# A two-block transformer kernel on one core: how five norm stages are computed, and what TensorE does while it waits in them

## Chip, core and metric

One Trainium2 core. The time is the device time of one execution in microseconds (us), the median of several. The kernel is one hand-scheduled program: each engine has its own instruction list, and all synchronisation is by counting semaphores.

## The reference, cut to what matters

Two blocks of two layers each, on 256 tokens ("LAT") of 1024 features, and from the second block on also on 256 context tokens. Every layer is: RMS norm, input projection, attention, output projection added to the tokens; then RMS norm, a wide feed-forward (2 x 2816 columns, a convolution over the tokens, a gate), and a down projection added to the tokens. What the change touches is the norm:

```python
y = x * rsqrt(mean(x * x) + eps) * g          # block 1 and its two layers
y = rms_norm(x, g) * (1 + scale) + shift      # block 2
```

All arithmetic is fp32. Each matrix product is made of three: both factors are split into a rounded part ("high") and the rest ("low"), and TensorE adds high*high, high*low and low*high.

## The kernel before

Weights stream from HBM in tiles of 1 MB into a ring of three slots. SyncE (SP) issues the transfers; the transfer into a slot waits until TensorE has read what was there. Each slot is handled in halves of 128 x 1024: ScalarE rounds a half into one of four high buffers (L334, helper `ahead`), GpSimd then writes the rest over the raw weights in place (L341), TensorE waits for that (L314) and multiplies (L347 to L349).

Five norms have no separate transposition stage and are called fronts here: the first layer's attention norm ("1.0 norm", behind the setup), "1.0 norm2", "1.1 norm", "1.1 norm2" and "2.1 norm2". All work on the two LAT tiles. A front runs like this:

- TensorE transposes the raw tokens into PSUM banks 4 to 7 (`turn_x_T`, L421; in the setup `first_T`, L1879). Feature tile k of 8 lies at `turned_k(k)`: 128 features by 256 tokens.
- ScalarE sums the squares of each token in two halves and takes two square roots (L464), one column per token tile; VectorE adds the first sum and eps before that (L437).
- TensorE spreads the two columns of roots over the 128 partitions, by a product with the identity into bank 3 (L430).
- VectorE inverts that 128 x 256 square (L439) into SBUF ("spread").
- For each k, VectorE multiplies bank, gain and spread into one of two SBUF buffers `TMP` (L446), ScalarE rounds that to the high part (L469; with a shift L471), and VectorE subtracts to get the low part (L454; with a shift L456). In order on VectorE: features 0, features 1, low 0, features 2, low 1, and so on. ScalarE also converts weight halves between these (`ahead` at L473 and L475).
- TensorE begins the next stage with k = 0 as soon as low 0 is there and waits for every low k in its first pass. In the feed-forward (`up_T`, L1226) this first pass is 48 products of 256 columns for two weight halves at once; in the projections (`in_T`) it is one column cut, half by half.

TensorE's instruction list is in program order; whatever stands in it ahead of a product is done before it. In the setup, SP issues the first three weight tiles, the gains, then 25 small loads (L2501) and the context tokens; ScalarE issues the identity and the tokens. The fourth weight tile waits for TensorE's reading of the first slot, and behind it on SP stand 16 small transfers (L1951) before the fifth tile.

## Time and profile before

| | us |
|---|---|
| median of 3 runs (1991.78 to 1992.41) | 1992.14 |
| the profiled execution | 1989.65 |
| its span, first to last instruction | 1987.9 |
| PE (TensorE matmul) busy | 1815.2 (91%) |
| POOL (GpSimd) / ACT (ScalarE) / DVE (VectorE) busy | 937.0 / 878.6 / 734.7 |
| mean granted TensorE clock, as a share of full speed | 0.942 |

The profiled execution is 2.49 us under the median of the three runs and its span 1.75 us under its own time. Busy time counts an engine with any instruction in flight; what an engine waited for is in the rows that follow below. The page also has the granted clock in 40 slices: it is 9 tenths or more in 36 of them.

### The profile page before, as it was taken

Reading aid. Unit: us, or ns where it says so; the run is one execution under the profiler, and the core shown is the slowest. Engines: PE = TensorE matmul, PEld = TensorE weight load, DVE = VectorE, ACT = ScalarE, POOL = GpSimd, SP = SyncE. Lnnn points to the kernel's source line nnn. Section 1 sums busy time; section 2 is a strip of 40 time slices with the busy share of each in tenths; the row PEclk is TensorE's granted clock in tenths of the full one; section 3 lists DMA queues with packets and bytes.
Section 4 is the critical chain, followed back from the end, with each engine's and each line's share of the span. In section 5 each row is a group of like instructions: output and inputs, shape, how many; then the busy total and the mean of one; then the engine's idle time right before and its main releaser. Section 6 shows DMA issues by size and latency. Waiting matters only on the chain.

```text
span 1987.9 us, 25834 instructions
## 1 busy us (share of the span) xinstructions
PE 1815.2 (91%) x10196; PEld 1463.2 (74%) x10196; DVE 734.7 (37%) x1591; ACT 878.6 (44%) x1542; POOL 937.0 (47%) x408
## 2 busy tenths in 40 slices
PE   5898999989789999789789999999999798889998
PEld 4667887867578878678544577888878686669986
DVE  4433223145432222464455425344311343344431
ACT  3655444345644443333324534444422255556653
POOL 3644676865356657333102023444434161138876
PEclk9999999999889999899875999999999899999999
DMA  5425997543169964222100022333323431126654
GB/s 192 148 86 182 305 308 264 170 149 127 64 208 304 307 240 166 69 85 85 43 0 1 1 85 64 88 103 99 92 80 105 102 106 43 43 85 170 182 160 146
DMA packets 257402, 261.36 MB, mean 131 GB/s; under 512 B 11123, under 2 KB 201811, under 8 KB 251011
## 3 DMA queue, kind: packets, MB, share of 16 engines
q1 hardware_dynamic: 256867, 258.61, 41.2%
q8 instruction: 81, 1.33, 0.3%
q10 hardware_dynamic: 416, 1.11, 0.1%
q14 instruction: 38, 0.31, 0.0%
HBM read 258.66 MB, written 1.05 MB: 131 GB/s over the span
## 4 chain that ended last, share of the span: by engine, by line
PE 78%; DVE 8%; ACT 5%; DMA 5%; issue 2%; POOL 1%; SPq 1%; ACTq 0%; DVEq 0%
PE bank L347 21%; PE bank L348 20%; PE bank L349 20%; PE bank L1382 2%; PE bank L719 2%; PE bank L1031 2%; PE bank L742 2%; ACT weights_high L334 1%; ACT work L1149 1%; PE bank L1001 1%; PE bank L1733 1%; DMA work<-in_ada_w 1%; PE bank L727 1%; DVE work L1110 1%; DMA weights<-in_hyb_w_in 1%
## 5 line engine op out<-in xcount | busy, mean ns | idle before, releaser
L341 POOL TENSOR_TENSOR weights_low<-weights,weights_high 128x1024 fp32r<-128x1024 f32 (+1 forms) x388 | 918.5, 2384 | 939.4 <-ACT weights_high L334 938.9
L334 ACT ACTIVATE weights_high<-weights 128x1024 fp32r<-128x1024 f32 (+1 forms) x388 | 401.0, 1045 | 477.1 <-PE bank L349 143.1
L347 PE MATMUL bank<-normed_features_high,weights_high 128*128 128x256 f32 (+1 forms) x1408 | 444.7, 316 | 13.3 <-DVE normed_features_low L454 6.7
L348 PE MATMUL bank<-normed_features_high,weights_low 128*128 128x256 f32 (+1 forms) x1408 | 439.4, 312 | 0.0
L349 PE MATMUL bank<-normed_features_low,weights_high 128*128 128x256 f32 (+1 forms) x1408 | 439.3, 312 | 0.0
L347 PE MATMUL bank<-weights_high,normed_features_high 128*128 128x512 f32 (+4 forms) x752 | 294.1, 391 | 34.9 <-POOL weights_low L341 10.8
L347 PEld LDWEIGHTS bank<-normed_features_high,weights_high 128*128 128x128 f32 x1408 | 272.2, 193 | 65.6 <-issue 35.4
L349 PEld LDWEIGHTS bank<-normed_features_low,weights_high 128*128 128x128 f32 x1408 | 272.0, 193 | 14.0
L348 PEld LDWEIGHTS bank<-normed_features_high,weights_low 128*128 128x128 f32 x1408 | 272.3, 193 | 13.6
L348 PE MATMUL bank<-weights_high,normed_features_low 128*128 128x512 f32 (+4 forms) x752 | 278.5, 370 | 0.0
L349 PE MATMUL bank<-weights_low,normed_features_high 128*128 128x512 f32 (+4 forms) x752 | 278.4, 370 | 0.0
L347 PEld LDWEIGHTS bank<-weights_high,normed_features_high 128*128 128x128 f32 x752 | 148.6, 198 | 70.8 <-issue 23.5
L347 PE MATMUL bank<-weights_high,hidden_high 128*128 128x512 f32 x440 | 175.6, 399 | 3.5 <-DVE hidden_low_narrow L1280 2.2
L349 PE MATMUL bank<-weights_low,hidden_high 128*128 128x512 f32 x440 | 173.0, 393 | 0.0
L349 PEld LDWEIGHTS bank<-weights_low,normed_features_high 128*128 128x128 f32 x752 | 148.5, 197 | 21.6
L348 PEld LDWEIGHTS bank<-weights_high,normed_features_low 128*128 128x128 f32 x752 | 149.1, 198 | 17.2
L1289 DVE SCALAR_TENSOR_TENSOR qk_features<-bank,convcol,qk_features 128x255 f32<-128x255 f32 x88 | 42.4, 482 | 213.1 <-ACT qk_features L1269 211.5
L347 PEld LDWEIGHTS bank<-weights_high,hidden_high 128*128 128x128 f32 x440 | 83.9, 191 | 28.9 <-DVE hidden_low_narrow L1280 4.7
L348 PE MATMUL bank<-weights_high,hidden_low_narrow 128*128 128x512 f32 x264 | 104.7, 397 | 0.0
L349 PEld LDWEIGHTS bank<-weights_low,hidden_high 128*128 128x128 f32 x440 | 83.9, 191 | 18.3
L583 DVE TENSOR_TENSOR bank<-bank,gate_rows 128x512 f32<-128x512 f32 x20 | 13.9, 696 | 209.5 <-PE bank L349 209.5
L1275 ACT ACTIVATE hidden_high<-bank 128x256 fp32r<-128x256 f32 (+1 forms) x88 | 38.6, 438 | 114.4 <-DVE bank L1318 81.0
(296 smaller groups left out, 2054.1 us busy)
## 6 DMA issues: line engine op xcount, KB each, us to landing
work<-in_ada_w SPq DMA_DIRECT2D x48, 1024.0 KB, 8.2
weights<-in_ffn_w_up SPq DMA_DIRECT2D x44, 1024.0 KB, 6.2
weights<-in_ffn_up SPq DMA_DIRECT2D x44, 1024.0 KB, 6.0
weights<-in_ffn_w_down SPq DMA_DIRECT2D x20, 1024.0 KB, 5.0
weights<-in_ffn_down SPq DMA_DIRECT2D x20, 1024.0 KB, 5.0
weights<-in_diff_w_qkv SPq DMA_DIRECT2D x12, 1024.0 KB, 5.1
weights<-in_hyb_w_in SPq DMA_DIRECT2D x11, 1024.0 KB, 5.4
weights<-in_odd_w_in SPq DMA_DIRECT2D x9, 1024.0 KB, 5.3
```

The source lines that it names most:

```text
L334: A.eng.activation(high(whigh[:, m % HIGHS, :]), raw(wslot[:, u % SLOTS, :]), ACT.Copy).then_inc(scalar_done, A.one(("A", "high", m)))
L341: G.eng.tensor_tensor(raw(wlow[:, u % SLOTS, :]), raw(wslot[:, u % SLOTS, :]), high(whigh[:, m % HIGHS, :]).bitcast(F32), ALU.subtract).th ...
L347: T.eng.matmul(out_, lh, rh, start=first, stop=False)
L348: T.eng.matmul(out_, ll, rh, start=False, stop=False)
L349: return T.eng.matmul(out_, lh, rl, start=False, stop=last)
L719: i = T.eng.matmul(bank[:, a:b], l, r, start=(m == 0), stop=(m == len(terms) - 1))
L727: i = T.eng.transpose(psum[3 + q % 2][:, c * P:(c + 1) * P], PB[q % NB][:, c * P:(c + 1) * P], ident)
L742: i = T.eng.matmul(o, l, r, start=(first and c == 0), stop=(last and c == nc_ - 1))
L1031: i = T.eng.matmul(psum[SCORES[x]][:, a:b], l, r, start=(m == 0), stop=(m == len(terms) - 1))
L1275: A.eng.activation(hidh(f, n), up_hidden(ph, f, n), ACT.Copy).then_inc(scalar_done, A.one(("A", ph, "high", f)))
L1289: V.eng.scalar_tensor_tensor(out=c[:, back:n], in0=g[:, 0:n - back], scalar=tap(2 - back, f), in1=c[:, back:n], op0=ALU.mult, op1=ALU.add) ...
L1382: i = T.eng.matmul(psum[4 + g][32 * j:32 * j + 2 + 2 * layer, :], (silu_below if layer else silu_c)[:, k, :], w[:, j * 512:(j + 1) * 512], ...
```

## The change

Three things, and one of the setup's loads:

- The two columns of roots are inverted first, by VectorE on 128 x 2 ("inverse"), and TensorE spreads the inverses. What VectorE then does with the square is a copy instead of an inversion. TensorE's spreading waits for VectorE instead of ScalarE.
- The features stay in the banks: VectorE writes the product back to `turned_k(k)`, and rounding and subtraction read it there. `TMP` is no longer used in fronts, and the wait for low k - 2 goes.
- TensorE multiplies the identity by itself into a bank that nobody reads: 5 products (2 in the setup) ahead of the wait for the inverse and 8 behind the spreading, plus 5 and 6 around the transposes of the setup.
- In the setup the tokens come in two transfers, one ahead of the weights on SP and one on ScalarE's queue, and ScalarE converts the first weight half right after the roots, the next three after k = 1, 3 and 5 (before: after k = 0, 2, 4 and 6).

```diff
+        def warm_T(T, bank, count):
+            for _ in range(count):
+                T.eng.matmul(psum[bank][:, 0:P], ident, ident, start=True, stop=True)
 def front_T(T, ph, x_ph):
             if x_ph != "setup":
                 turn_x_T(T, ph, x_ph, 1)
-            T.eng.wait_ge(scalar_done, done("A", ph, "root"))
+            if x_ph not in ("setup", "1.0 ffn down", "1.1 ffn down"):
+                T.eng.wait_ge(scalar_done, done("A", x_ph, "squares", 1))
+            idle_bank = 1 if x_ph == "setup" else 2 if x_ph.endswith("down") else 0
+            warm_T(T, idle_bank, 2 if x_ph == "setup" else 5)
+            T.eng.wait_ge(vector_done, done("V", ph, "inverse"))
             for j in range(2):
                 i = T.eng.matmul(psum[SPREAD][:, j * P:(j + 1) * P], stat[:, 24 + j:25 + j].to_broadcast([P, P]), ident, start=True, stop=True)
             i.then_inc(tensor_done, T.one(("T", ph, "rstd")))
+            warm_T(T, idle_bank, 8)
 def front_V(V, ph, x_ph, which):
+            V.eng.wait_ge(scalar_done, done("A", ph, "root"))
+            V.eng.reciprocal(stat[:, 24:26], stat[:, 24:26]).then_inc(vector_done, V.one(("V", ph, "inverse")))
             V.eng.wait_ge(tensor_done, done("T", ph, "rstd"))
-            V.eng.reciprocal(spread[:, 0:SEQ], psum[SPREAD][:, 0:SEQ]).then_inc(vector_done, V.one())
+            V.eng.tensor_copy(spread[:, 0:SEQ], psum[SPREAD][:, 0:SEQ]).then_inc(vector_done, V.one())
...
-                    if k >= 2:
-                        V.eng.wait_ge(vector_done, done("V", ph, "low", k - 2))
-                    V.eng.scalar_tensor_tensor(out=TMP[k % 2][:, 0:SEQ], in0=turned_k(k), scalar=a, in1=spread[:, 0:SEQ],
+                    V.eng.scalar_tensor_tensor(out=turned_k(k), in0=turned_k(k), scalar=a, in1=spread[:, 0:SEQ],
...
-                        V.eng.tensor_tensor(nTl[:, q, span(LAT)], TMP[q % 2][:, 0:SEQ], high, ALU.subtract)
+                        V.eng.tensor_tensor(nTl[:, q, span(LAT)], turned_k(q), high, ALU.subtract)
 def front_A(A, ph, x_ph, which, next_ph):
+            if x_ph == "setup":
+                ahead(A, first_half[next_ph] + 1)
...
-                if x_ph == "setup" and k in (0, 2, 4, 6):
-                    ahead(A, first_half[next_ph] + 1 + k // 2)
+                if x_ph == "setup" and k in (1, 3, 5):
+                    ahead(A, first_half[next_ph] + 2 + k // 2)
 def first_T(T):
             T.eng.wait_ge(ident_in, 16)
-            T.eng.wait_ge(x_in, 16)
+            warm_T(T, 1, 5)
+            T.eng.wait_ge(x_in, 16 * 2)
...
+            warm_T(T, 1, 6)
             T.eng.wait_ge(first_in, 16)
 sync:
+            sp.dma_start(xt[:, 2, :], io["x"][0][0:P, :]).then_inc(x_in, 16)
 scalar:
-            act.dma_start(xt[:, 2:4, :], io["x"][0].rearrange("(t p) d -> p t d", p=P)).then_inc(x_in, 16)
+            act.dma_start(xt[:, 3, :], io["x"][0][P:2 * P, :]).then_inc(x_in, 16)
```

## Rows read from the trace of the kernel before

**Rows 1.** The page, part 4: the chain that ended last, shares by engine.

```profile
PE 78%; DVE 8%; ACT 5%; DMA 5%; issue 2%; POOL 1%; SPq 1%; ACTq 0%; DVEq 0%
```

**Rows 2.** Windows: length, each engine's busy us (records), clock, DMA share, GB/s.

```profile
180.00:182.00 2.00, 2.00 (x12) 2.00 (x11) 1.89 (x6) 1.13 (x3) 0.00 (x0) 0.50 1.02 422
...
578.00:724.00 146.00, 146.00 (x1185) 124.60 (x1184) 41.47 (x91) 69.73 (x106) 100.79 (x43) 1.00 0.92 299
```

**Rows 3.** Chain of waits, the first 80 us: start, length, engine, tile, line.

```profile
1.22 8.38 DMA x_tokens<-in_x
9.73 3.65 PE bank L1879 x16
...
15.71 1.77 DVE spread_rstd L439
...
19.72 2.38 DVE normed_features_low L454
...
29.77 4.48 DVE normed_features_low L454 x2
...
37.89 0.39 SPq L2496
...
49.40 5.21 DMA weights<-in_hyb_w_in
```

**Rows 4.** Timeline of the first front: start, length, instruction, idle time before it.

```profile
13.31 0.28 PE L1882 MATMUL bank<-con,work 16*128 16x16 f32 x1
...
13.91 0.48 ACT L464 ACTIVATE stat<-stat 128x1 f32<-128x1 f32 x2 [1.31 <-DVE stat L437]
...
19.46 4.84 POOL L341 TENSOR_TENSOR weights_low<-weights,weights_high 128x1024 fp32r<-128x1024 f32 x2 [19.02 <-ACT weights_high L334]
...
21.86 0.58 PE L347 MATMUL bank<-weights_high,normed_features_high 128*128 128x256 f32 x1 [6.19 <-POOL weights_low L341]
```

**Rows 5.** VectorE by line and form: busy us, mean ns; or ns minimum/median/maximum.

```profile
L1105 DVE RECIPROCAL mxs<-mxs 128x2 f32<-128x2 f32 x48 | 8.0, 166 | 47.4 <-ACT work L1149 47.4
L894 DVE COPY big<-bank 128x256 f32<-128x256 f32 x5 | 2.1, 425 | 16.0 <-PE bank L349 16.0
```

**Rows 6.** Answers on single lines: ns minimum/median/maximum, first and last start.

```profile
L454 DVE TENSOR_TENSOR normed_features_low<-gate_rows,normed_features_high x32: 412/417/2562, 18.5 to 575.2; 128x256 fp32r<-128x256 f32 x32
L1280 DVE TENSOR_TENSOR hidden_low_narrow<-bank,hidden_high x66: 412/415/425, 196.8 to 1917.9; 128x256 fp32r<-128x256 f32 x66
L1296 DVE TENSOR_TENSOR bank<-bank,qk_features x44: 431/433/433, 192.0 to 730.3; 128x256 f32<-128x256 f32 x44
```

**Rows 7.** Timeline of the second front, from the spreading to its first pass's end.

```profile
175.39 0.71 PE L430 MATMUL bank<-con,stat 128*128 128x128 f32 x4 [1.26 <-ACT stat L464]
...
177.93 0.88 DVE L446 SCALAR_TENSOR_TENSOR gate_rows<-bank,veccol,spread_rstd 128x256 f32<-128x256 f32 x2
...
184.59 0.43 DVE L454 TENSOR_TENSOR normed_features_low<-gate_rows,normed_features_high 128x256 fp32r<-128x256 f32 x1 [0.15 <-ACT normed_features_high L469]
...
186.12 0.28 PE L347 MATMUL bank<-normed_features_high,weights_high 128*128 128x256 f32 x1
186.24 0.28 PE L348 MATMUL bank<-normed_features_high,weights_low 128*128 128x256 f32 x1
...
188.00 1.04 PE L1382 MATMUL bank<-work,st 128*2 128x512 f32 x8
```

**Rows 8.** Timeline: fronts three, four and five.

```profile
423.07 0.19 PEld L347 LDWEIGHTS bank<-weights_high,normed_features_high 128*128 128x128 f32 x1 [0.23 <-POOL weights_low L341]
...
568.57 0.88 DVE L446 SCALAR_TENSOR_TENSOR gate_rows<-bank,veccol,spread_rstd 128x256 f32<-128x256 f32 x2
...
577.97 1.04 PE L1382 MATMUL bank<-work,st 128*4 128x512 f32 x8
...
1782.61 0.88 DVE L446 SCALAR_TENSOR_TENSOR gate_rows<-bank,acol,spread_rstd 128x256 f32<-128x256 f32 x2
...
1792.40 1.06 ACT L334 ACTIVATE weights_high<-weights 128x1024 fp32r<-128x1024 f32 x1 [1.67 <-PE bank L349]
```

More of the change, by code:

```diff
@@ L453, in front_V @@
                     if b is None:
-                        V.eng.tensor_tensor(nTl[:, q, span(LAT)], TMP[q % 2][:, 0:SEQ], high, ALU.subtract).then_inc(vector_done, V.one(("V", ph, "low", q)))
+                        V.eng.tensor_tensor(nTl[:, q, span(LAT)], turned_k(q), high, ALU.subtract).then_inc(vector_done, V.one(("V", ph, "low", q)))
                     else:
-                        V.eng.scalar_tensor_tensor(out=nTl[:, q, span(LAT)], in0=TMP[q % 2][:, 0:SEQ], scalar=b, in1=high,
+                        V.eng.scalar_tensor_tensor(out=nTl[:, q, span(LAT)], in0=turned_k(q), scalar=b, in1=high,
                                                    op0=ALU.add, op1=ALU.subtract).then_inc(vector_done, V.one(("V", ph, "low", q)))
@@ L468, in front_A @@
                 if b is None:
-                    A.eng.activation(nTh[:, k, span(LAT)], TMP[k % 2][:, 0:SEQ], ACT.Copy).then_inc(scalar_done, A.one(("A", ph, "high", k)))
+                    A.eng.activation(nTh[:, k, span(LAT)], turned_k(k), ACT.Copy).then_inc(scalar_done, A.one(("A", ph, "high", k)))
                 else:
-                    A.eng.activation(nTh[:, k, span(LAT)], TMP[k % 2][:, 0:SEQ], ACT.Identity, bias=b).then_inc(scalar_done, A.one(("A", ph, "high", k)))
-                if x_ph == "setup" and k in (0, 2, 4, 6):
-                    ahead(A, first_half[next_ph] + 1 + k // 2)
+                    A.eng.activation(nTh[:, k, span(LAT)], turned_k(k), ACT.Identity, bias=b).then_inc(scalar_done, A.one(("A", ph, "high", k)))
+                if x_ph == "setup" and k in (1, 3, 5):
+                    ahead(A, first_half[next_ph] + 2 + k // 2)
                 if x_ph != "setup" and k % 4 == 3:
@@ L1893, in first_A @@
             A.eng.activation(stat[:, 32:33], lam[:, 6:7], ACT.Sqrt).then_inc(scalar_done, A.one())
-            A.eng.wait_ge(x_in, 16)
+            A.eng.wait_ge(x_in, 16 * 2)
             for t in LAT:
```

## Prediction

> **What bounds the kernel now.** I read the chain of waits first, by engine [rows 1]: TensorE holds 78% of it, so what matters is where TensorE stands still or runs slowly. The windows over a feed-forward's first half [rows 2] show it busy for all of 146 us at full clock: whatever a stage gains ahead of such a stretch is kept, because nothing in the stretch is late. The idle lies in the five fronts, and there the chain goes over VectorE. In the first front [rows 3] it runs from the tokens' transfer (1.22 + 8.38 = 9.60) through transposes, spreading and the 1.77 us inversion into the subtractions of L454. Four entries of that line (the two shown, and 2.00 and 2.42 us between them) hold 11.28 us for five instructions, while the line's median is 0.417 us [rows 6]. The timeline [rows 4] has GpSimd's L341 running beside them, 4.84 us for two. At the other fronts [rows 7, 8] the same steps are short, but TensorE then works at half clock: granted 0.50 in 180:182 [rows 2], after it had stood idle from 176.10 to 179.47.
>
> **The cost of a front's head.** Behind the roots stood spreading (0.71 us) and an inversion of 1.76 us. Now: an inversion of 128x2 (0.166 us) [rows 5] with about 0.05 us for the extra hand-over, the same spreading, a copy of 128x256 from a bank (0.425 us) [rows 5]. 1.76 - 0.22 - 0.43 = 1.1 us earlier, at each front. TensorE's new wait for "squares 1" holds up nothing: that sum is made from the first half's columns, long before the roots. Behind the wait for the inverse stand the spreading, the fillers and the first products, all of which need it anyway.
>
> **The fillers.** The spreading is two such products and shows four records in 0.71 us [rows 7], so I take 0.3 us a product at full clock, and at half clock twice the transposes' 3.65 / 16 = 0.228 us a record [rows 3], 0.46. Five ahead of the spreading: about 1.5 us, against 1.26 us of idle [rows 7] plus the 0.22 us inversion; they fit within 0.1 us, and by 0.2 us they don't in the third front, where the last transposes end later. Eight behind it: 2.4 us, from 176.3 to 178.7 in the second front, with low 0 ready at 178.2. That overrun of 0.5 us costs nothing where VectorE's rhythm sets the pace: 0.85 us per feature tile against 6 x 0.12 = 0.71 us for six products at full clock [rows 7]. Bounds of the fillers: nothing at best, 1.2 us a front if they run at half clock and nothing comes of it.
>
> What they should buy is the clock. With them TensorE never stands for long between the last transposes and the first product, so I expect it to stay at full clock; no row shows a stretch filled with such products, only that idle came before the fall. Bounds: nothing, and the whole slow stretch. I take the whole, since the fillers are dense.
>
> **Features in the banks.** VectorE's multiplication gets a bank as output: L1296, bank to bank, takes 0.433 us [rows 6], so nothing is lost. The subtraction now has one operand in a bank, exactly L1280's form: 0.415 us, at most 0.425 in 66 instances all over the program, much of it beside GpSimd, where L454 with two SBUF operands reached 2.562 [rows 6]. I take 0.415 us and no collisions; the bounds are that and today's collisions.
>
> Here a rule of the Trainium skill speaks against the change. Its page "VectorE: DVE Perf Modes", section on the TRN2 errata, gives an instruction that reads PSUM 62 cycles more fixed cost than one from SBUF, at 0.96 GHz 65 ns. By it the forty subtractions, eight in each of five fronts, would be slower by 2.6 us in all, and the time by as much at most. The rows 412/417 from SBUF and 412/415 from a bank don't show that difference for this form, so I leave it out; it lies within the range.
>
> **Front one.** Its steps, in the trace's clock:
> - Tokens: on ScalarE's queue 0.56 MB instead of 1.06 MB is ahead of their end. In proportion 8.38 us becomes 4.4, landing at 5.6; as some of it is fixed I take 6.6. Bounds 5.4 and 9.6. The first weights come 0.5 MB later, and are not needed before 13.
> - Transposes until 10.3, as slowly as now. Six fillers, 1.8 to 2.7 us: the gains' transpose starts at 12.5 instead of 13.31 [rows 4]. The fillers stand in front of it, so most of the transfer's gain is spent there.
> - From there to the end of the roots stays 1.1 us: 13.6 (now 14.39). Inverse 0.22, spreading 1.0, copy 0.5: the first multiplication at 15.3 instead of 17.5, 2.2 us earlier (bounds 1.1 and 3.5).
> - First weight half: 13.6 + 1.05 + 2.42 = 17.1; TensorE starts there instead of at 21.86.
> - In the second front low 7 ends 7.1 us after the first multiplication (177.93 to 185.02) [rows 7]. Three conversions of 1.05 us between ScalarE's roundings add 0.5 us each (bounds 0 and 1.05): low 7 at 23.9. Then 15 products are left, 1.8 us at full clock: 25.7. Today SP issues the fourth weight tile 0.2 us behind that point, at 37.89 [rows 3]; it would be 25.9. Gain 12.0 us.
>
> Checked by parts: the head 2.2, the collisions 11.28 - 5 x 0.415 = 9.2, half clock on 15 products 1.4, less what the conversions add. All that follows hangs on that issue: 16 small transfers, then the fifth tile at 49.40 [rows 3], for which TensorE waits. So it all moves by 12.0. SP is free of its small loads by then (the last is issued at 21.1 now, half a microsecond later after).
>
> **Fronts two to five.**
> - Two: low 7 at 185.02 - 1.1 = 183.9, six products 0.7, end of the first pass 184.6 instead of 188.0 [rows 7]: 3.4 us.
> - Four: 568.57 - 1.1 + 7.1 + 0.7 = 575.3 instead of 577.97 [rows 8]: 2.7 us.
> - Five, whose tiles with a shift need 7.7 us: 1782.61 - 1.1 + 7.7 + 0.7 = 1789.9 instead of 1792.4 [rows 8]: 2.5 us.
> - Three is a projection of 512 columns, TensorE's own pace counts, and its fourth weight half ended the wait at 423.07 [rows 8]. One collision (2.0 us) and 0.9 of the head go from that half's path; TensorE, started at 412.1 with 36 products of 0.229 us at full clock, is there at 420.35. 2.7 us.
>
> Sum: 12.0 + 3.4 + 2.7 + 2.7 + 2.5 = 23.3 us. The profiled execution's 1989.65 becomes 1966.3; from the median of the runs, 2.5 us above it, 1968.8. I forecast 1968.8.
>
> **Rivals.**
> - A, the fillers don't hold the clock. For it: no row shows identity products doing so. Against: the clock fell only where TensorE stood. Fronts two, four and five gain 1.1 each, three 0.9, one 10.5 (the last 15 products are slow): 14.7 us, 1977.4.
> - B, the collisions stay: it was not the second SBUF operand. For it: GpSimd writes SBUF just when VectorE does. Against: L1280's maximum. Front one 12.0 - 9.2 = 2.8, three 0.9, the others as forecast: 12.3 us, 1979.8.
> - C, the first front's gain is given back in the first layer's attention, because a transfer or the small loads are late instead. For it: the queue is full until 28. Against: the chain through SP's issue is relative. Half of 12 lost: 1974.8.
> - D, the other side: VectorE writes a bank while ScalarE reads the next and TensorE a third, and each of the 80 VectorE instructions in fronts gets slower by contention in PSUM. It decides from 23.3 / 80 = 0.29 us each; at 0.4 us it is 8.7 us slower, 2000.8. Against it: L1296's 431 to 433 ns with TensorE busy all the time.
>
> **How the numbers follow.** Forecast 0.70, A 0.14, B 0.03, C 0.09, D 0.03, and 0.01 that nothing changes. The forecast's own range is 1964 to 1974: the head's bounds (-1.3, +1.1), the conversions (-1.5, +1.6), the page's 2.6, the fillers' overruns. A, B and C lie below 1980, so 1963.5 to 1980 leaves D and the tails out. A measurement of this kernel tells 0.2%, 4 us, from no change. Faster by more 0.95, within it 0.02, slower 0.03.
>
> **What would show it.** L454 without any instance above 0.5 us; L439 five times 0.43; SP's fourth weight tile issued near 26; the granted clock 1.00 through fronts two to five, and first passes 3.4, 2.7, 2.5 us shorter counted from the roots' end. Wrong would be: a clock of 0.50 behind the fillers (A), a subtraction of 2 us beside L341 (B), a new wait of TensorE between 26 and 150 (C), multiplications well over 0.48 us (D).

## The result, and the profile after

The changed kernel takes 1958.97 us (median of 4 runs, 1956.30 to 1962.88) where the one before takes 1991.96 us (4 runs, 1989.74 to 1992.41). The ratio is 0.9838, 95% interval 0.9820 to 0.9856. The forecast was 1968.8 us with a range from 1963.5 to 1980: the direction, the places and the mechanism came out, but the gain is 33.0 us and not 23.3, and the time lies below the range.

The profiled execution of the changed kernel was the slowest of its four (1962.88 us, span 1961.1 us). The same kernel profiled again (experiment e1) has a span of 1958.5 us. Both stand in the table further down.

The chain of waits of the changed kernel, shares by engine (the page, part 4), to be set beside [rows 1]:

```profile
PE 79%; DVE 8%; ACT 5%; DMA 4%; issue 2%; POOL 1%; SPq 1%; DVEq 0%; ACTq 0%
```

TensorE sets the end as before. What was taken away lay in the fronts. Windows over fronts two to five of the changed kernel (length, TensorE's, its loads', VectorE's, ScalarE's and GpSimd's busy us with records, granted clock, DMA share, GB/s):

```profile
160.00:170.00 10.00, 9.31 (x79) 8.71 (x81) 6.66 (x18) 5.22 (x14) 2.35 (x2) 1.00 0.89 311
389.00:400.00 11.00, 10.76 (x63) 9.41 (x64) 6.98 (x19) 7.04 (x16) 3.62 (x3) 1.00 0.28 102
544.00:554.00 10.00, 9.49 (x79) 9.14 (x78) 6.66 (x18) 5.27 (x15) 2.35 (x2) 1.00 0.92 315
1755.00:1764.00 9.00, 7.59 (x60) 7.21 (x61) 7.46 (x17) 4.15 (x12) 2.01 (x1) 1.00 0.42 117
```

The clock is 1.00 in all four; before, it was 0.50 in the middle of the second front [rows 2]. Over the whole kernel before, the page has 9 tenths or more in 33 of the 40 slices, not in 36 as said above.

The first front of the changed kernel, from its timeline (start, length, instruction, idle before it), beside [rows 3, 4]:

```profile
4.35 2.50 PE bank L414 x10
6.84 2.67 PE bank L1892 x16
...
10.79 0.23 PE L1896 MATMUL bank<-con,work 16*128 16x16 f32 x1
...
11.34 0.48 ACT L474 ACTIVATE stat<-stat 128x1 f32<-128x1 f32 x2 [2.04 <-DVE stat L447]
11.86 0.17 DVE L449 RECIPROCAL stat<-stat 128x2 f32<-128x2 f32 x1 [0.55 <-ACT stat L474]
...
12.83 0.42 DVE L451 COPY spread_rstd<-bank 128x256 f32<-128x256 f32 x1 [0.80 <-PE bank L439]
13.29 0.88 DVE L456 SCALAR_TENSOR_TENSOR bank<-bank,veccol,spread_rstd 128x256 f32<-128x256 f32 x2
...
15.26 0.39 PE L347 MATMUL bank<-weights_high,normed_features_high 128*128 128x256 f32 x1 [0.69 <-POOL weights_low L341]
15.61 11.84 POOL L341 TENSOR_TENSOR weights_low<-weights,weights_high 128x1024 fp32r<-128x1024 f32 x5 [0.41 <-ACT weights_high L334]
...
19.06 0.81 DVE L464 TENSOR_TENSOR normed_features_low<-bank,normed_features_high 128x256 fp32r<-128x256 f32 x2
22.01 1.21 SPq L2511 DMA_DIRECT2D weights<-in_hyb_w_in  x1
```

Three things are to be seen. The narrow inverse and the copy stand where the 1.77 us inversion stood. GpSimd works from 15.61 to 27.45 without a break, and the subtractions beside it (L464) take their 0.42 us all the same. SP issues the fourth weight tile at 22.01 instead of 37.89 [rows 3].

The changed kernel's front instructions on VectorE (ns minimum/median/maximum, first and last start), beside [rows 6]:

```profile
L464 DVE TENSOR_TENSOR normed_features_low<-bank,normed_features_high x32: 411/415/426, 14.2 to 552.6; 128x256 fp32r<-128x256 f32 x32
L456 DVE SCALAR_TENSOR_TENSOR bank<-bank,veccol,spread_rstd x32: 480/483/493, 13.3 to 551.7; 128x256 f32<-128x256 f32 x32
L451 DVE COPY spread_rstd<-bank x5: 424/425/425, 12.8 to 1758.6; 128x256 f32<-128x256 f32 x5
```

The worst subtraction fell from 2562 to 426 ns; its median, 417 from SBUF and 415 from a bank, did not move.

Where the time went, for the profiled executions that bear on the change. Each front is measured from the end of its square roots to a fixed landmark behind it: SP's issue of the tile behind the first pass (fronts one, three, five), or TensorE's first modulation product (two, four). "Outside" is all the rest of the span, "head" the start of the program up to the first roots' end.

| kernel | head | front 1 | 2 | 3 | 4 | 5 | outside | span |
|---|---|---|---|---|---|---|---|---|
| before | 14.39 | 23.50 | 12.66 | 12.30 | 12.00 | 12.68 | 1900.4 | 1987.9 |
| after | 11.82 | 10.19 | 8.89 | 8.71 | 8.89 | 9.46 | 1903.1 | 1961.1 |
| e1 the same again | 13.55 | 10.18 | 8.89 | 8.74 | 8.88 | 9.47 | 1898.8 | 1958.5 |
| e2 no fillers | 12.31 | 11.64 | 11.47 | 10.13 | 10.22 | 10.55 | 1900.0 | 1966.3 |
| e3 with the wait | 12.68 | 10.69 | 9.61 | 8.80 | 9.61 | 10.23 | 1900.8 | 1962.4 |
| e4 features in SBUF | 12.38 | 18.24 | 9.64 | 8.84 | 9.65 | 10.25 | 1903.8 | 1972.8 |
| e5 wide inverse | 13.44 | 11.32 | 10.02 | 9.99 | 10.02 | 10.60 | 1898.6 | 1964.0 |
| e6 one tokens' load | 16.30 | 10.18 | 8.88 | 8.70 | 8.90 | 9.46 | 1899.3 | 1961.7 |
| e7 banks alone | 14.50 | 14.77 | 12.49 | 11.45 | 12.07 | 12.53 | 1906.5 | 1984.3 |
| e9 four conversions | 12.68 | 13.33 | 8.88 | 8.71 | 8.89 | 9.45 | 1893.9 | 1955.8 |

The fronts repeat to 0.05 us between two executions of one kernel; the head and what lies outside do not. So a part of the change is read from its front's column, and the total from the medians. The profiled executions differ from the medians by up to 4 us: from the one before to the two after, the span falls by 26.8 and 29.4 us.

### The profile page after: what moved, and what is told of

Its sections match the earlier page's. It is cut to its first block, busy times and chain, and to the rows that moved or that the text cites. A ratio compares the mean times of both kernels' runs of the same rounds, so it can differ in the third digit from the quotient of the medians.

```text
span 1961.1 us, 26131 instructions
## 1 busy us (share of the span) xinstructions
PE 1822.8 (93%) x10342; PEld 1471.6 (75%) x10342; DVE 712.7 (36%) x1596; ACT 876.4 (45%) x1542; POOL 936.3 (48%) x408
## 3 DMA queue, kind: packets, MB, share of 16 engines
HBM read 258.66 MB, written 1.05 MB: 132 GB/s over the span
## 4 chain that ended last, share of the span: by engine, by line
PE 79%; DVE 8%; ACT 5%; DMA 4%; issue 2%; POOL 1%; SPq 1%; DVEq 0%; ACTq 0%
PE bank L347 22%; PE bank L348 21%; PE bank L349 20%; PE bank L1394 2%; PE bank L731 2%; PE bank L754 2%; PE bank L1043 2%; ACT work L1161 1%; ACT weights_high L334 1%; PE bank L1013 1%; PE bank L1745 1%; DMA work<-in_ada_w 1%; DVE work L1122 1%; PE bank L739 1%; PE bank L402 1%
## 5 line engine op out<-in xcount | busy, mean ns | idle before, releaser
L348 PEld LDWEIGHTS bank<-normed_features_high,weights_low 128*128 128x128 f32 x1408 | 268.9, 191 | 13.6
```

Of the source, the lines that this page charges most:

```text
L348: T.eng.matmul(out_, ll, rh, start=False, stop=False)
```

## Experiments

Each kernel is the changed one with the edit shown, if nothing else is said, and each was timed against the kernel before on the same chip.

**e1: the changed kernel again.** The spread of its four runs was wider than that of the kernel before.

> The changed kernel once more, nothing edited. Theory: its gain over the kernel before is about 28.7 us in the five fronts, the same in every execution, and a rest that goes up and down with where TensorE's clock falls elsewhere. So single executions spread over 1956 to 1963 us as the first four did, and a longer one has a lower mean granted clock (0.948 went with 1962.9, 0.951 with 1956.3). Rival: the 1962.9 us of the profiled execution was one stall of another kind, and these lie within 1 us of 1959 whatever their clock.

Measured: 1959.59 us (1958.02 to 1962.36), ratio 0.9844 (0.9829 to 0.9858). The gain is real and repeats. The first four runs of the changed kernel, with mean granted clocks of 0.948, 0.949, 0.950 and 0.951, took 1962.88, 1959.18, 1958.76 and 1956.30 us: 0.003 of 1960 us is 5.9 us of clock, and the times differ by 6.6. In the two profiled executions the granted clock stands at 0.50 for 207.3 and 201.8 us from the first front on, none of it in the fronts, and what lies outside takes 1903.1 and 1898.8 us. Work done in 5.5 us at half clock takes 2.7 us at full (an estimate), so the clock accounts for more than half of these 4.3 us; the rest is not placed.

**e2: no fillers.** TensorE still waits at the same places but multiplies nothing there.

```diff
 def warm_T(T, bank, count):
-            for _ in range(count):
-                T.eng.matmul(psum[bank][:, 0:P], ident, ident, start=True, stop=True)
+            return
```

> All identity products left out, everything else as changed. Theory: they are worth 5 to 6 us in the first front (transposes 3.65 instead of 2.88 us, spreading 1.2 instead of 0.7, the first pass at half clock, so that SP issues the fourth weight tile near 27.5 instead of 22.0) and 1.5 to 2.7 us in each of the fronts two, four and five, about 12 us in all: 1971 us. Rival 1: they hold no clock and only fill, 1959 us. Rival 2: they lift the clock outside the fronts as well, then 1974 us or more.

Measured: 1970.97 us (1968.10 to 1979.36), ratio 0.9906 (0.9883 to 0.9930). Windows over its second front (length, TensorE's busy us, clock, DMA share, GB/s), and its first product there:

```profile
160.00:164.00 4.00, 0.97 (x7) 0.95 0.94 263
164.00:168.00 4.00, 3.37 (x16) 0.50 1.02 405
```

```profile
164.63 0.55 PE L347 MATMUL bank<-normed_features_high,weights_high 128*128 128x256 f32 x1 [2.01 <-DVE normed_features_low L463]
```

TensorE stands for 1.65 us ahead of the spreading and 2.01 us behind it, and then works at 0.50. The fronts grow by 1.5, 2.6, 1.4, 1.3 and 1.1 us, 7.9 in all. The total of 11.4 us between the medians came out as expected, its division did not: I had expected 5 to 6 us of it in the setup and the first front. The front is 1.5 us longer, and the head is shorter without the fillers: in e1 and in e2 both token tiles have landed at 7.50 and 7.51 us, and the roots end at 13.55 with fillers and at 12.31 without. So all 21 fillers of the setup together bring 0.2 us, and what they are worth lies in fronts two to five, 6.4 us. The profiled span is 7.8 us longer than e1's; what is left of the 11.4 is not placed.

**e3: the dropped wait put back.** The features stay in the banks, but tile k waits again for the subtraction of tile k - 2, which nothing needs there.

```diff
                     a, b = which(k, 1)
+                    if k >= 2:
+                        V.eng.wait_ge(vector_done, done("V", ph, "low", k - 2))
                     V.eng.scalar_tensor_tensor(out=turned_k(k), ...)
```

> Features in the banks as changed, but VectorE again waits for low k - 2 ahead of features k. Theory: the wait on the instruction just issued costs VectorE about 0.12 us per feature tile (rhythm 0.85 instead of 0.72 us), of which TensorE hides a part: 0.5 us in each of fronts two, four and five, about 1 us in the first, 1961.5 us. Rival: the shorter rhythm comes from bank operands and the wait costs nothing, 1959 us and a rhythm of 0.72 us.

Measured: 1963.59 us (1962.70 to 1966.77), ratio 0.9865 (0.9851 to 0.9880). VectorE in the second front of e3, and below it in the changed kernel:

```profile
163.71 0.41 DVE L466 TENSOR_TENSOR normed_features_low<-bank,normed_features_high 128x256 fp32r<-128x256 f32 x1
164.16 0.49 DVE L458 SCALAR_TENSOR_TENSOR bank<-bank,veccol,spread_rstd 128x256 f32<-128x256 f32 x1
164.56 0.41 DVE L466 TENSOR_TENSOR normed_features_low<-bank,normed_features_high 128x256 fp32r<-128x256 f32 x1
```

```profile
164.02 0.41 DVE L464 TENSOR_TENSOR normed_features_low<-bank,normed_features_high 128x256 fp32r<-128x256 f32 x1
164.35 0.48 DVE L456 SCALAR_TENSOR_TENSOR bank<-bank,veccol,spread_rstd 128x256 f32<-128x256 f32 x1
164.75 0.42 DVE L464 TENSOR_TENSOR normed_features_low<-bank,normed_features_high 128x256 fp32r<-128x256 f32 x1
```

With the wait the multiplication starts 0.45 us after the subtraction's start, without it 0.33 us, before the subtraction has ended. One tile takes 0.85 us with it and 0.73 without: 0.12 us a tile, and 0.5, 0.7, 0.1, 0.7 and 0.8 us at the five fronts. In the order of VectorE's list low k - 2 stands directly ahead of features k, so the wait is for the engine's own last instruction. It looked free, since the two run one behind the other anyway; it is not, since it keeps the next instruction from starting under the last one's end.

**e4: the features in SBUF again.** Multiplication to the old pair of buffers, with the wait they need; inverse, fillers, tokens and conversions as changed. Against e3 it differs in the place of the features alone.

```diff
-                    V.eng.scalar_tensor_tensor(out=turned_k(k), ...)
+                    if k >= 2:
+                        V.eng.wait_ge(vector_done, done("V", ph, "low", k - 2))
+                    V.eng.scalar_tensor_tensor(out=TMP[k % 2][:, 0:SEQ], ...)
...
-                        V.eng.tensor_tensor(nTl[:, q, span(LAT)], turned_k(q), high, ALU.subtract)
+                        V.eng.tensor_tensor(nTl[:, q, span(LAT)], TMP[q % 2][:, 0:SEQ], high, ALU.subtract)
...
```

> Features in the two SBUF buffers again (with the wait for low k - 2 that these need); spreading, fillers, transfers and conversions as changed. Theory: the subtractions with two SBUF operands meet GpSimd again, 2 us each, three to five times in the first front and once in the third: 8 to 10 us more than with the wait alone, 1971 us. Rival: with the new order of the conversions GpSimd no longer runs beside them and the time is that of the kernel with the wait alone, 1961.5 us.

Measured: 1973.89 us (1972.12 to 1974.54), ratio 0.9911 (0.9895 to 0.9928). The subtraction's line in e4 and its worst two beside GpSimd in the first front:

```profile
L466 DVE TENSOR_TENSOR normed_features_low<-gate_rows,normed_features_high x32: 413/416/2412, 14.8 to 564.0; 128x256 fp32r<-128x256 f32 x32
```

```profile
16.48 2.34 DVE L466 TENSOR_TENSOR normed_features_low<-gate_rows,normed_features_high 128x256 fp32r<-128x256 f32 x1
...
21.08 2.40 DVE L466 TENSOR_TENSOR normed_features_low<-gate_rows,normed_features_high 128x256 fp32r<-128x256 f32 x1
```

With both operands in SBUF the stalls are back, and the first front is 18.24 instead of 10.69 us: 7.55 us for the operand's place. Fronts two to five don't differ from e3's by more than 0.05 us. The expected collision in the third front is there, 2.41 us beside GpSimd, but it costs no more than 0.04 us: TensorE's own pace bounds that front once the clock is full.

**e5: the wide inverse.** Roots are spread first, and the inverse taken of 128x256.

```diff
-            T.eng.wait_ge(vector_done, done("V", ph, "inverse"))
+            T.eng.wait_ge(scalar_done, done("A", ph, "root"))
...
-            V.eng.wait_ge(scalar_done, done("A", ph, "root"))
-            V.eng.reciprocal(stat[:, 24:26], stat[:, 24:26])...
...
-            V.eng.tensor_copy(spread[:, 0:SEQ], psum[SPREAD][:, 0:SEQ])...
+            V.eng.reciprocal(spread[:, 0:SEQ], psum[SPREAD][:, 0:SEQ])...
```

> The changed kernel, but the roots are spread first and the inverse is taken of the spread 128x256 (as before the change), instead of 128x2 ahead of the spreading and a copy behind it; banks, fillers, tokens and conversions stay. Theory (the head's 1.1 us of the prediction counts once in each front): 1.76 us for 0.17 + 0.42 us and a hand-over of 0.05 us, so 1.1 us later in each of five fronts, 5.5 us: 1965 us, with the granted clock still 1.00 through fronts two to five, because eight products behind the spreading still leave only about 1 us of standing. Rival (the narrow inverse also keeps the standing short enough for the clock): the clock falls behind the eight products, and each front is 2.3 to 2.6 us longer: 1971 us.

Measured: 1966.08 us (1964.80 to 1967.09), ratio 0.9886 (0.9866 to 0.9905). The fronts are 1.14, 1.13, 1.25, 1.14 and 1.13 us longer, 5.8 in all. TensorE stands 1.56 us behind its fillers instead of 0.23, but the clock holds (second front of e5, same columns as for e2):

```profile
158.00:170.00 12.00, 10.10 (x79) 1.00 0.76 263
```

**e6: one transfer for both token tiles**, on ScalarE's queue as before.

```diff
-            sp.dma_start(xt[:, 2, :], io["x"][0][0:P, :]).then_inc(x_in, 16)
...
-            act.dma_start(xt[:, 3, :], io["x"][0][P:2 * P, :]).then_inc(x_in, 16)
+            act.dma_start(xt[:, 2:4, :], io["x"][0].rearrange("(t p) d -> p t d", p=P)).then_inc(x_in, 16)
```

> The changed kernel, but both token tiles come with one transfer on ScalarE's queue, behind the identity, as before the change. Theory (in the changed kernel the tokens' landing, near 6.3 us, sets the start of ScalarE's squares and so the roots): tokens at 9.6 us, the roots end near 14.4 instead of 11.8, and all behind moves by 2.6 us: 1962 us. Rival (the fillers and the first weight half set the first front's start, as the prediction had it for most of this gain): at most 1 us, 1960 us.

Measured: 1963.78 us (1961.33 to 1967.08), ratio 0.9876 (0.9854 to 0.9898). TensorE in e6's first front:

```profile
9.81 3.67 PE L1892 MATMUL bank<-con,x_tokens 128*128 128x128 f32 x16 [2.56 <-DMA x_tokens<-in_x]
...
13.27 2.06 PE L414 MATMUL bank<-con 128*128 128x128 f32 x12
15.26 0.23 PE L1896 MATMUL bank<-con,work 16*128 16x16 f32 x1
```

The roots end at 16.30 us, 1.9 us later than in the kernel before, though the tokens land at about the same time (9.76 and 9.60 us). The six fillers stand in front of the gains' transpose (L1896), and VectorE adds eps, for which the roots wait, only behind its copy of the gains. They take 2.06 us here, partly at half clock. They are not free when the tokens come early either: TensorE in e1, and below it in e2, without fillers and with the tokens landing at the same time.

```profile
7.55 3.68 PE L1892 MATMUL bank<-con,x_tokens 128*128 128x128 f32 x16 [0.22 <-DMA x_tokens<-in_x]
11.02 1.57 PE L414 MATMUL bank<-con 128*128 128x128 f32 x12
12.52 0.23 PE L1896 MATMUL bank<-con,work 16*128 16x16 f32 x1
```

```profile
7.65 3.65 PE L1891 MATMUL bank<-con,x_tokens 128*128 128x128 f32 x16 [7.65 <-DMA x_tokens<-in_x]
11.22 0.28 PE L1895 MATMUL bank<-con,work 16*128 16x16 f32 x1
```

The fillers put the gains' transpose off by 1.30 us, and the five ahead of the tokens did not speed up the transposes there (3.68 and 3.65 us). All behind the head is as in the changed kernel. The head is 2.7 to 4.5 us longer than in the changed kernel's two executions, where the expectation had 2.6: 2.3 to 3.5 us by the later landing, the rest by fillers and, against one of the two, transposes that run slower. No run leaves out these six alone.

**e7: the kernel before, with the banks alone.** Only the place of the features and the dropped wait are changed; head, inverse, tokens and conversions are the old ones, and there are no fillers.

> The kernel before, with one part of the change alone: the features stay in their banks (the multiplication writes where it read, and the wait for low k - 2 goes). Head, inverse, tokens, conversions and fillers are as before. Theory (the parts are not additive: with TensorE at half clock the shorter rhythm of the features is hidden behind its products): only the first front's collisions and 0.5 us of its rhythm are gained, 8 to 9 us: ratio to before 0.9957, 1982.5 us. Rival (the parts add up): 0.7 us of rhythm at three more fronts as well, 10.4 us: 1980.5 us.

Measured: 1983.99 us (1973.46 to 1986.14, 10 runs), ratio 0.9971 (0.9953 to 0.9988). Windows over e7's second, third and fourth front:

```profile
174.80:188.00 13.20, 13.20 (x97) 0.86 0.53 173
407.00:420.00 13.00, 12.70 (x49) 0.86 0.25 81
565.00:578.00 13.00, 11.67 (x78) 0.77 0.52 196
```

The first front is 8.73 us shorter, the third 0.85, the second and fifth by no more than 0.17, the fourth not at all: with TensorE partly at half clock the faster rhythm of VectorE waits for it. The parts are not additive, as expected. The fronts gain 9.8 us, but the medians differ by 5.9 only: the profiled execution has 6 us more outside the fronts than that of the kernel before, more than any other in the table; why is open.

**e9: four conversions between the roundings**, as before the change. (e8 is told of below.)

```diff
-            if x_ph == "setup":
-                ahead(A, first_half[next_ph] + 1)
...
-                if x_ph == "setup" and k in (1, 3, 5):
-                    ahead(A, first_half[next_ph] + 2 + k // 2)
+                if x_ph == "setup" and k in (0, 2, 4, 6):
+                    ahead(A, first_half[next_ph] + 1 + k // 2)
```

> The changed kernel, but ScalarE makes the first four weight conversions behind its roundings of tiles 0, 2, 4 and 6 of the first front, as before the change, not one of them ahead of the first rounding and three behind 1, 3 and 5. Theory (what is left of the first front's 13.3 us when the collisions, the inverse, the fillers and the dropped wait are taken off, about 2 us, is this move): the fourth weight tile is issued about 2 us later counted from the roots' end, 1961.5 us. Rival (ScalarE's four conversions take the same time wherever they stand, and the rest of the first front's gain is an interaction of the other parts): at most 0.5 us later, 1959.5 us.

Measured: 1959.10 us (1955.06 to 1964.40), ratio 0.9846 (0.9805 to 0.9887). TensorE in its first front:

```profile
18.48 0.39 PE L347 MATMUL bank<-weights_high,normed_features_high 128*128 128x256 f32 x1 [3.05 <-POOL weights_low L341]
...
20.46 0.42 PE L349 MATMUL bank<-weights_low,normed_features_high 128*128 128x256 f32 x1
```

The front is 3.15 us longer: the first weight half is ready 5.80 us behind the roots' end instead of 3.44, TensorE stands for 3.05 us, and from 20.0 to 23.4 us its products go at half clock (0.42 us a record instead of 0.28). The expected 2 us were the start alone; the clock came on top. The median doesn't show these 3 us: the runs spread over 9 us, and this profile has 5 us less outside the fronts than e1's, with 11 us less at half clock there. The part is shown by its column, its worth in the total is not.

**e8: fillers in the third layer's attention.** The profile of the changed kernel still has TensorE at 0.50 for 60 us there, while it is busy. This asks whether the change's own means work at another place: one identity product behind each of the scores.

```diff
                     i.then_inc(tensor_done, T.one(("T", ph, "scores", s)))
+                    warm_T(T, 7, 1)
```

> The changed kernel with one more identity product (128x128 by 128x128, into bank 7, which nobody reads then) behind each of the scores of the softmax attention of the third layer. There TensorE is busy nearly all the time from 1016 to 1077 us, with half-size products (64 rows or 64 columns), and the granted clock is 0.50. Theory (a full-size product among the others brings the clock up, as it does in the fronts): the 61 us shorten to about 35 to 40, less 33 products of 0.25 us: 1942 us. Rival (the clock stays at 0.50, since a busy TensorE did not raise it): 33 products at 0.25 to 0.5 us are added to a stretch that TensorE bounds: 1971 us.

Measured: 1976.27 us (1972.98 to 1979.98), ratio to the kernel before 0.9938 (0.9917 to 0.9960), 17 us slower than the changed kernel. That stretch in e1 and in e8 (length, TensorE's busy us, clock, DMA share, GB/s):

```profile
1016.00:1076.00 60.00, 57.72 (x154) 0.50 0.00 1
```

```profile
1012.00:1077.00 65.00, 65.00 (x181) 0.50 0.00 1
```

TensorE is busy for all of 65 us and the clock stays at 0.50. The Trainium skill, page "TensorE: Matmul & The Clock Gate", section "Part 1: The HAM clock gate", has activity release the clock; busy time alone did not here. The theory fell: one filler behind each score does not bring the clock back in this stretch; they were only added to it.

**e10: fillers where TensorE stands, ahead of that stretch.** 34 products ahead of the third layer's cell, 7 (3 in the first head) and 3 inside its heads, 10 behind its last sums, 4 behind each of the attention's first four scores.

> The changed kernel with identity products at the standing places of the third layer's cell and ahead of its attention: 34 ahead of the cell's first products, where TensorE stands for 9.2 us, 7 (3 in the first head) ahead of each third product of queries and keys, where it stands for 2.0 us, 3 ahead of the sums, 10 behind the last sums, where it stands for 2.6 us, and 4 behind each of the first four scores of the attention. All go into banks that nobody reads then. Theory (the clock falls where TensorE stands, and in the attention it stays at 0.50 only because it came in at 0.50): the cell's 38 us at low clock end, about 5 us a head and 3 for the first, less overruns: 12 to 18 us; and the attention's 61 us become 40 to 45: together 1925 to 1935 us. Rival (the attention's half-size products let the clock fall by themselves, however TensorE comes in): the cell's part alone, 1942 to 1948 us. Second rival (VectorE's and ScalarE's chain bounds both stretches at once when TensorE is faster, so the fillers stand in the way): 1955 to 1962 us.

Measured: 1955.28 us (1951.60 to 1960.21), ratio 0.9823 (0.9789 to 0.9858). Two rows of its timeline:

```profile
948.53 10.08 PE L414 MATMUL bank<-con 128*128 128x128 f32 x68 [4.99 <-ACT big L577]
...
1026.60 0.44 PE L740 MATMUL bank<-con,work 128*128 128x128 f32 x2 [1.42 <-DVE work L793]
```

The 34 products stood behind the wait for the phase before, began 4.99 us late and partly at half clock, and pushed the cell back by 5.8 us. The heads of the cell ran at 1.00. The cell with the standing ahead of it takes 70.7 us instead of 75.1, the attention with its turns 97.4 instead of 99.4; the theory's 12 to 18 and 16 to 21 us did not come. The attention came in at 1.00, with fillers up to 1021.2 us. From there it had none, TensorE stood for 1.42 us up to 1026.6, and from 1028 to 1072 the clock was at 0.50 again. The fillers' end and the standing come together, so this run doesn't tell which of them lost the clock. The time lies in the second rival's range, but what the profile shows is late fillers and a lost clock.

**e11: the same, dense.** The products stand ahead of the wait, and the attention has 4, 3, 2 or 1 behind each score down to the 18th.

```diff
         phase("2.0 mlstm",
+              lambda T: (T.eng.wait_ge(scalar_done, done("A", "2.0 in", "piece", 18)),
+                         warm_T(T, 4, 36), fence(T, "2.0 in"), mlstm_T(T, "ml")), ..., no_fence="T")
...
+                    warm_T(T, 7, 4 if s < 4 else 3 if s < 7 else 2 if s < 16 else 1 if s < 18 else 0)
```

> The run before put its 34 products behind the wait for the phase before, so they began 5 us late, at half clock, and pushed the cell back by about 6 us; and its attention came in at full clock but fell to 0.50 behind a standing of 1.4 us at the eighth score. Here 36 products stand ahead of that wait, 6 and 2 in the heads, 10 behind the last sums, and in the attention 4 behind each of scores 0 to 3, 3 behind 4 to 6, 2 behind 7 to 15, 1 behind 16 and 17. Theory (standing alone makes the clock fall, and a stretch that is kept without it stays at 1.00): the cell takes 65 us instead of 75, the attention's steps about 2.1 us instead of 2.8 (16 of them) and 2.7 instead of 4.2 (7 of them), 20 us: 1930 us. Rival (the attention's half-size products cannot carry the clock, so it falls between 1025 and 1040 all the same): 1945 us, or later by the fillers at half clock.

Measured: 1941.68 us (1939.29 to 1943.12), ratio 0.9756 (0.9741 to 0.9770): faster than both kernels, 17 to 18 us below the changed one. Windows over the cell and the attention, and where the clock was lost:

```profile
939.00:1003.00 64.00, 59.12 (x360) 1.00 0.05 17
1004.00:1064.00 60.00, 58.13 (x289) 0.91 0.00 1
```

```profile
1044.68 0.78 PE L755 MATMUL bank<-work,big 128*64 128x128 f32 x4 [1.68 <-ACT work L828]
```

The cell with the standing ahead of it takes 64.4 us instead of 75.1, the attention with its turns 89.8 instead of 99.4. It gains 18 us and not the expected 29. The cell gave its 10. The 16 narrow steps of the attention gave 7 us instead of 11: up to the fourth score the fillers cost 2.0 us, and from there a step takes about 2.1 us, as expected. The wide steps gave 2.5 us instead of 10, because at the change of tile width TensorE stood for 1.68 us and the clock fell once more, for 10 us. Here too the last fillers ended just before, at 1040.8 us, so the rival (these products can't carry the clock by themselves) is not excluded. The clock came back at 1055.3 us without any filler, 2.8 us after the first eight records in a row of L755; in e1 it came back 2.7 us after the same place in the attention, at 1076.1.

**e12: e11, and 7 fillers ahead of each full norm's transposes.**

> The same, and 7 products ahead of the transposes of each of the three full norms, where TensorE stands for 4 to 9 us and the transposes then run at half clock (32 records in 6.13 us). Theory (7 dense products, 2 to 3 us, bring the clock up before or during the transposes, and VectorE's part of the norm takes as long as they do): 1.5 to 2 us at each of three norms, 1925 us, or 5 us below the run beside it. Rival (what is gained in the transposes is waited for at the first features, since VectorE sets that chain): the same time as the run beside it.

Measured: 1940.99 us (1938.83 to 1942.59), ratio 0.9751 (0.9734 to 0.9767). The transposes of the second such norm in e11 and in e12:

```profile
1145.11 6.50 PE L402 MATMUL bank<-con,work 128*128 128x128 f32 x32 [3.99 <-DVE work L395]
```

```profile
1149.64 4.33 PE L403 MATMUL bank<-con,work 128*128 128x128 f32 x32
```

They take 2.2 us less, but from the last product ahead of the norm to the first behind it only 1.0 us is gained (12.7 to 11.7). At the other two norms it is 0.8 (17.7 to 17.0) and 0.4 us (16.0 to 15.6), 2.2 us in all: less than half of the theory's 4.5 to 6, but not the rival's nothing. The medians differ by 0.7 us, less than their spread.

## Why the prediction came out as it did

The mechanism was right part by part; what failed were sizes, all in the same direction: VectorE's rhythm without the wait (0.73 us a tile, not 0.85), the conversions between ScalarE's roundings (0.3 us in all, not 1.5), and TensorE's start in the third front (0.85 us too late). Less what erred the other way they make 4.5 us of the 9.7 by which the gain was missed; 0 to 1.8 us more came in the head, and the rest is open.

**What bounds, and where.** Right. The fronts' columns went from 87.5 us (head included) to 58.0 and 59.7; that is 27.8 to 29.6 us of the 33.0. In the stretches between, the largest change is 1.6 us, behind the first front (see C below).

**The head, 1.1 us at each front.** Right to 0.1 us: e5 gives 1.13 to 1.25.

**The fillers hold the clock.** Right (1.00 in all fronts; 0.50 without them in e2), and rival A is out. e2 puts them at 7.9 us in the fronts, less 1.2 us that they cost in the head.

**No collisions.** Right, and rival B is out: 7.55 us by e4 against e3, on the operand's place alone. The prediction had 9.2 for the first front's stalls, five of them. With the conversions in their new order four subtractions of e4 meet GpSimd there (1.24, 2.34, 2.40 and 2.07 us); in the old order e7 gains 8.73, rhythm included. The Trainium skill, page "SBUF — State Buffer", section "Who interferes with whom", has VectorE and GpSimd share a pair of ports under an exclusive lock, which a VectorE instruction with two SBUF inputs needs against a GpSimd instruction that reads SBUF; the later one waits for the whole of the other. This case's traces agree: 2.34 and 2.40 us beside GpSimd's 2.36 us instructions with two, at most 0.426 with one.

**The page against the change.** The prediction weighed the Trainium skill's "VectorE: DVE Perf Modes", section on the TRN2 errata: 65 ns more for an operand in PSUM. No run here shows it: 415 ns from a bank, 416 and 417 from SBUF, in the same form. The measurement decides.

**The dropped wait: the step that failed in fronts two, four and five.** The prediction named the wait in its diff and priced nothing for it; it took "VectorE's rhythm" of "0.85 us per feature tile" over into the changed kernel, and "low 7 ends 7.1 us after the first multiplication". The rhythm is 0.73, and low 7 ends 6.3 us after (162.35 to 168.6 in the second front). e3 puts the wait at 0.7, 0.1, 0.7 and 0.8 us. Forecast for fronts two to five: 3.4, 2.7, 2.7 and 2.5 us. Measured: 3.8, 3.6, 3.1 and 3.2. The rhythm's 0.8 us shows only in part because another term errs the other way: behind low 7 the prediction had 0.7 us ("six products"), and it is 1.1 to 1.2. In the third front the wait is not the cause (0.1 us by e3). There the prediction had TensorE "started at 412.1", 3.8 us behind the roots' end at 408.28; measured are 2.97, and these 0.85 us are the whole miss. It gives no working for 412.1. Its price of 0.3 us a filler puts the eight behind the spreading at 2.4 us, and they take 1.95; so the mis-sized term is at least in part the fillers' price. From its start TensorE needs 8.3 us for 36 products, as the prediction had. The one collision that it took off this front's path is worth nothing there with a full clock (e4).

**The first front: the terms that were mis-sized.** From the roots' end the prediction had the first product 3.5 us later and the issue 12.3 us later (13.6 to 25.9). Measured are 3.44 and 10.19. The 2.1 us between are, first, "three conversions of 1.05 us between ScalarE's roundings add 0.5 us each", 1.5 us. They add 0.3 in all: the eight low tiles end 6.6 us after the first multiplication's start (13.29 to 19.87), against 6.3 in the second front. Second, the rhythm again, 7.1 to 6.3, of which e3 alone shows 0.5 in this front. What the prediction left without a term is that the conversion ahead of the first rounding keeps TensorE from standing between the fillers and the first weight half, 0.69 us instead of 3.05: e9 puts the whole move at 3.15 us. It had the first product's time right, but not that the old order would have cost the clock with it.

**The head of the program.** Forecast: roots end at 13.6. Measured: 11.82 in one execution, 13.55 in the other, with the tokens landing at 6.3 and 7.5 us (7.8 in e5). The first is 0.5 us below the step's bounds (12.3 to 14.7), the second within; the transfers' landing is not reproducible to better than 1.5 us. The transposes ran at 0.18 us a record in the first of these and at 0.23, as before, in the second, though five fillers had gone ahead of them in both.

**Fitting it together.** 23.3 forecast; 2.4 more in fronts two to five; 2.1 more in the first front; 0 to 1.8 more in the head: 27.8 to 29.6 us, as the columns show. The rest of the 33.0, some 3 to 5 us, is not shown by any profile: outside head and fronts the changed kernel's two profiled executions are 2.7 us longer and 1.6 us shorter than the one before, and two executions of one kernel differ there by 4.3 us (e1). In e1 the difference of the medians was 31.4 us. So how the last 3 to 5 us came about stays open, and part of them may be luck. The range's lower end was 5 us below the forecast; it allowed the head and the conversions to go well, but put no bound on the rhythm and none on what lies outside.

**The other rivals.** C: the stretch from the fourth weight tile's issue to the second front's roots took 137.5 us and takes 138.9 and 139.0, so up to 1.6 us were given back, but not by a late transfer: TensorE's waits over 0.4 us in it add up to 10.1 us before and to 10.3 and 9.4 after, while its mean clock went from 0.985 to 0.975 and 0.963. D: the multiplications took 484 ns and take 483, so no price for reading and writing the banks at once shows.

## What to carry to other kernels

A wait on the engine's own last instruction is not free even when nothing seems to be waited for: here it cost 0.12 us for each, 0.5 to 0.8 us a front where VectorE set the pace and 0.1 where TensorE did. So look for such waits before taking a rhythm over. Where the clock has fallen, look at the standing time ahead of the slow stretch and fill that, densely and ahead of any wait. One filler behind each score inside the slow stretch only lengthened it (e8); one to four behind a score, in a stretch that came in at full clock, went with a clock that stayed (e11). A filler ahead of something that is waited for costs its own time: the six ahead of the gains' transpose cost 1.2 us, and all 21 of the setup together brought 0.2 us. Keeping one operand of VectorE in a bank was worth 7.55 us where GpSimd worked beside it and VectorE set the pace, and nothing in a front that TensorE bounds.

## What the runs showed of the hardware that was not expected

- TensorE was busy for 65 of 65 us at a granted clock of 0.50 (e8), in products with 64 rows or 64 columns mixed with full ones. In e10 and e11 the same kinds of products, with fillers among them for the first 7 and 37 us, ran at 1.00 for 14 and 41 us after coming in at 1.00. In both the clock fell shortly after the fillers had ended and TensorE had stood for 1.42 (e10) and 1.68 us (e11); the two are not separated.
- A clock can also survive standing: in e5 TensorE is idle for 1.9 of 12 us in the second front, 1.56 of them in one piece, and stays at 1.00. So the length of the standing alone doesn't decide.
- A 128x256 subtraction costs the same from a bank as from SBUF, 415 and 416 to 417 ns.
- The granted clock's mean differs by 0.003 between executions of one kernel on one core, and the time by 6.6 us with it.
